# Turning the 64x64 blocks of a triangular inverse one by one instead of two heads at a time

## The chip, the cores and the metric

The kernel runs on one core of a Trainium2 chip. The metric is the device time of one execution in microseconds; of several runs the median is taken. The engines are named as the profile names them: PE is the tensor engine (PEld its weight loads, PE its matmuls), DVE the vector engine, ACT the scalar engine, POOL GpSimd, SP the engine that issues most of the DMAs. Matmuls write to PSUM, which here is eight banks of 128 partitions by 512 float32 columns, named L0 to L3 and Q0 to Q3.

## The reference, cut to what matters

The reference is one transformer block of each of two kinds, applied to 256 tokens of width 1024 in float32. Nearly all of its arithmetic is in products with weight matrices. The change sits in one small part of the first block, the chunked gated delta rule of 8 heads, which solves a lower triangular system for every chunk of 64 tokens:

```python
decay = jnp.exp(jnp.where(causal, gc[..., :, None] - gc[..., None, :], -jnp.inf))
k_beta = k * beta[..., None]
a_low = jnp.where(strict, jnp.einsum("bhnid,bhnjd->bhnij", k_beta, k) * decay, 0.0)
t_mat = a_low + jnp.eye(L, dtype=f32)
rhs = jnp.concatenate([v * beta[..., None], k_beta * jnp.exp(gc)[..., None]], axis=-1)
sol = lax.linalg.triangular_solve(t_mat, rhs, left_side=True, lower=True, unit_diagonal=True)
...
def step(state, inp):
    v_new = u_i - jnp.einsum("bhld,bhde->bhle", w_i, state)
```

The kernel forms the inverse of the unit triangular matrix itself. It works on 128 tokens at once: first the inverses of the two 64x64 blocks on the diagonal, then, in a last level, the 64x64 block below them.

## The kernel before

**Weights.** The work is a fixed list of steps, and every engine's program walks that list. The weights come in units of 128x1024 float32 (512 KB). SP loads a unit into one of four `raw` buffers, ACT casts it to a high part `w_hi` (line 1325), POOL subtracts to get the low part `w_lo` (line 504), and PE multiplies in three products, high by high, high by low, low by high (lines 517 to 519). One unit in the column form is 12 matmuls of 128x512. A semaphore that PE raises tells ACT that a slot may be overwritten.

**Filling.** The small products of attention and of the delta rule depend on each other, with DVE and ACT between them. So PE's program puts weight units between them, by hand: `fill(step, i)` on PE runs the i-th unit of the steps listed for this place. For the inverse of head group 0 (step `("inv", 0)`) these are the units of `("z", 1)` and `("ga", 0)`, for group 1 those of `("gb", 0)` and `("gb", 1)`.

**The inverse.** Each of the two head groups has four heads (`GH`), two tiles of 128 tokens (`NT`, index t), and in each tile two diagonal blocks of 64 rows: partitions 0 to 63 and 64 to 127. `T[partition, t, head, 64]` holds both blocks of a head beside each other in the folded form: the upper partitions hold the second block. `Td` is the same, with each block transposed; `AT` is the transposed matrix itself. The levels l = 1 to 6 double the size of the finished blocks:

1. X = A T: PE, line 1097, sixteen 64x64 matmuls for both tiles (at the last level only the lower block's, eight). DVE masks the result into `X` (line 1910 through a helper; at the last level a plain copy).
2. From level 2 on, `turn_blocks` (line 1079) transposes T on PE, into the other two banks, and ACT copies the result to `Td` (at the last level to the diagonal blocks of `TT`). At level 1 it is instead the other way round, ahead of the loop: `Td` exists first, and the turn gives `T`.
3. A fill: one unit, 12 matmuls; at the last level half a unit, 6 matmuls.
4. PE waits for DVE's `X` and ACT's `TT` mark of this tile, and runs Y = T X (line 1113, sixteen matmuls with `Td` as stationary operand; at the last level line 1110, eight with `TT`).
5. DVE subtracts Y from T (line 1910), and PE's next level waits for it tile by tile.

`turn` is the tensor engine's transpose instruction, `mm` its ordinary matmul. In the kernel before, one turn takes two heads at a time: 128 partitions by 128 columns, of which the 128 columns are two heads of 64. Its result has the first head of the pair in partitions 0 to 63 and the second in 64 to 127, and the two blocks beside each other in the columns. `copy_blocks` on ACT puts this in place by four copies of 64 partitions by 128 elements (line 1609) for a tile.

Of the kernel before, what the change touches and what calls it, by code (L numbers as in the profile page):

```python
# [29 lines left out]
P = 128  # L30
# [5 lines left out]
GH = 4  # L36
# [7 lines left out]
HALF = P // 2  # L44
# [175 lines left out]
def build(nc, a, out, known):  # L220
# [30 lines left out]
    with ctx:  # L251
# [44 lines left out]
        T = big("T", 60, [P, NT, GH, HALF])  # L296
        Td = big("Td", 62, [P, NT, GH, HALF])
        TT = big("TT", 64, TOKENS)
# [20 lines left out]
        h = big("h", 28, [P, NT, D])  # L319
# [46 lines left out]
        ident, tri, ones = square(0), square(1), square(2)  # L366
# [63 lines left out]
        Q = [ctx.enter_context(nc.psum_tensor(f"Q{n}", [P, 512], F32)) for n in range(4)]  # L430
# [8 lines left out]
        AC = Done(scalar_done, known.get("act"))  # L439
# [72 lines left out]
        def _(pe):  # L512
            mm, turn = nc.tensor.matmul, nc.tensor.transpose
# [418 lines left out]
            for step in SCHEDULE:  # L932
                kind = step[0]
                if kind == "u":
# [8 lines left out]
                    for t in range(NT):  # L943
                        for j in range(4):
                            pe.wait_ge(*(VE(step, "scaled", 1, j) if t == 1 and j < 2 else AC(step, "scaled", t, j // 2)))
                            for i in range(2):
                                last = turn(Q[j][:, i * SEQ + t * P:i * SEQ + (t + 1) * P], xn0[:, t, (2 * j + i) * P:(2 * j + i + 1) * P], ident)
# [4 lines left out]
                elif kind == "ba":  # L952

                    pe.wait_ge(*VE(("u",), "split"))
                    for k in range(KD):
                        mm(Q[0][0:16, 0:SEQ], baH[:, k, :], uH[:, k, :], start=k == 0, stop=False)
                        mm(Q[0][0:16, 0:SEQ], baH[:, k, :], uL[:, k, :], start=False, stop=False)
                        last = mm(Q[0][0:16, 0:SEQ], baL[:, k, :], uH[:, k, :], start=False, stop=k == KD - 1)
                    last.then_inc(*PE.mark(step))
                elif kind == "rates":  # L960
                    pe.wait_ge(*VE(("ba",), "turned"))
                    for t in range(NT):
                        last = turn(Q[1][:, t * 16:t * 16 + 16], baT[0:16, t * P:(t + 1) * P], ident[0:16, 0:16])
# [6 lines left out]
                elif kind == "tok":  # L970
                    gr = step[1]
                    for part in range(3):
                        for t in range(NT):
                            b = part * NT + t
# [7 lines left out]
                            for i in range(GH):  # L982
                                last = turn(Q[b % 3][:, i * P:(i + 1) * P], C[:, part * GH + i, t * P:(t + 1) * P], ident)
# [3 lines left out]
                elif kind == "decay":  # L987
# [6 lines left out]
                    for t in range(NT):  # L994
                        last = mm(Q[3][:, t * 8:t * 8 + GH], tri, g[:, t * 8 + gr * GH:t * 8 + gr * GH + GH], start=True, stop=True)
# [6 lines left out]
                elif kind == "feat":  # L1002
# [4 lines left out]
                    src = {"kn": lambda t, i: tok[:, t, 1, i, :], "kb": lambda t, i: kb[:, t, i, :],  # L1007
                           "qn": lambda t, i: tok[:, t, 0, i, :], "qe": lambda t, i: qe[:, i, :]}
                    for b, (what, t) in enumerate(lots):
# [5 lines left out]
                        for i in range(GH):  # L1015
                            last = turn(Q[b % 3][:, i * P:(i + 1) * P], src[what](t, i), ident)
# [4 lines left out]
                    for t in range(NT):  # L1021
                        for i in range(GH):
                            last = mm(Q[2 * t + i // 2][:, (i % 2) * 256:(i % 2 + 1) * 256], kT[:, t, i, :],
                                      kbqT[:, t, i, :, :].rearrange("p a b -> p (a b)"), start=True, stop=True)
# [3 lines left out]
                elif kind == "att":  # L1028
                    gr = step[1]
                    for b in range(4):  # L1030
                        part, pair = b // 2, b % 2
                        pe.wait_ge(*VE(("moba", gr, part), "rope", 1))
                        pe.wait_ge(*VE(("feat", gr), "attn", 1, 1))
                        for i in range(2):
                            for t in range(NT):
                                last = turn(Q[b][:, i * SEQ + t * P:i * SEQ + (t + 1) * P], mtok[:, part, t, 2 * pair + i, :], ident)
# [3 lines left out]
                    for i in range(GH):  # L1040
                        last = mm(Q[0][:, i * P:(i + 1) * P], qTa[:, i, 0:P], kTa[:, i, 0:P], start=True, stop=True)
                    last.then_inc(*PE.mark(step, "scores", 0))
                    for i in range(GH):
                        last = mm(Q[1 + i // 2][:, (i % 2) * SEQ:(i % 2 + 1) * SEQ], qTa[:, i, P:SEQ], kTa[:, i, :], start=True, stop=True)
# [4 lines left out]
                    for b, j in enumerate((0, 1, 2)):  # L1049
# [3 lines left out]
                        for i in range(GH):  # L1053
                            last = turn(Q[b][:, i * P:(i + 1) * P], pr[:, i, j * P:(j + 1) * P], ident)
# [4 lines left out]
                    for i in range(GH):  # L1059
                        bank = Q[3 if i < 2 else 0]  # L1060
                        c0 = (i % 2) * SEQ
                        mm(bank[:, c0:c0 + SEQ], mtok[:, 2, 0, i, :], prT[:, i, 0:SEQ], start=True, stop=False)
                        last = mm(bank[:, c0 + P:c0 + SEQ], mtok[:, 2, 1, i, :], prT[:, i, SEQ:3 * P], start=False, stop=True)
# [4 lines left out]
                elif kind == "inv":  # L1068
                    gr = step[1]
                    fill(step, 0)  # L1070
                    diagonal = [slice(0, HALF), slice(HALF, P)]
# [2 lines left out]
                        return [bank[d, i * HALF:(i + 1) * HALF] for d in diagonal]  # L1074

                    def turn_blocks(bank, src, t):

                        for pair in range(2):
                            last = turn(bank[:, pair * P:(pair + 1) * P], src[:, t, 2 * pair:2 * pair + 2, :].rearrange("p h d -> p (h d)"), ident)
                        return last  # L1080

                    pe.wait_ge(*VE(step, "Td"))
# [4 lines left out]
                    for l in range(1, LEVELS):  # L1087
                        A = [Q[2], Q[3], Q[0], Q[1]] if l % 2 else Q
                        top = l == LEVELS - 1
                        for t in range(NT):  # L1090
                            pe.wait_ge(*(VE(step, "T", l - 1, t) if l > 1 else AC(step, "T", 0, t)))
                            for i in range(GH):
                                for b, d in enumerate(diagonal):
# [3 lines left out]
                                    last = mm(tiles(A[t], i)[b], AT[k, t, i, d], T[k, t, i, :], start=True, stop=True)  # L1097
# [5 lines left out]
                        for t in range(NT):  # L1103
# [3 lines left out]
                            for i in range(GH):  # L1107
                                if top:
                                    d = diagonal[1]
                                    last = mm(tiles(A[t], i)[0], X[d, t, i, :], TT[d, t, i, d], start=True, stop=True)  # L1110
                                else:
                                    for b, d in enumerate(diagonal):
                                        last = mm(tiles(A[t], i)[b], Td[d, t, i, :], X[d, t, i, :], start=True, stop=True)
                            last.then_inc(*PE.mark(step, "Y", l, t))
                elif kind == "scan":
# [4 lines left out]
                    for t in range(NT):  # L1120
                        for i in range(GH):
                            last = mm(Q[t][:, i * P:(i + 1) * P], TT[:, t, i, :], tok[:, t, 2, i, :], start=True, stop=True)
                        last.then_inc(*PE.mark(step, "u", t))
                    for i in range(GH):
                        last = mm(Q[2][:, i * P:(i + 1) * P], kbe[:, i, :], TT[:, 1, i, :], start=True, stop=True)
                    last.then_inc(*PE.mark(step, "wT"))
                    pe.wait_ge(*AC(step, "u", 0))
                    for i in range(GH):
                        last = mm(Q[3][:, i * P:(i + 1) * P], kdec[:, i, :], vn[:, 0, i, :], start=True, stop=True)
                    last.then_inc(*PE.mark(step, "S"))  # L1130
                    for i in range(GH):
                        last = mm(Q[0][:, i * P:(i + 1) * P], aT[:, 0, i, :], vn[:, 0, i, :], start=True, stop=True)
                    last.then_inc(*PE.mark(step, "o", 0))
                    pe.wait_ge(*AC(step, "S"))
                    for i in range(GH):
                        last = mm(Q[2][:, i * P:(i + 1) * P], wT[:, i, :], S[:, i, :], start=True, stop=True)
# [23 lines left out]
                elif kind == "ffn":  # L1160
# [10 lines left out]
                    if c > 0:  # L1171
                        prev = ("ffn", blk, c - 1)
                        pe.wait_ge(*VE(prev, "hidden", 1))
                        for j in range(2):
                            for i in range(2):
                                for t in range(NT):
                                    last = turn(Q[2 * (c % 2) + j][:, i * SEQ + t * P:i * SEQ + (t + 1) * P],  # L1177
                                                hm[:, t, (2 * j + i) * P:(2 * j + i + 1) * P], ident)
# [3 lines left out]
                elif kind == "down":  # L1182
# [5 lines left out]
                    for k in range(KF - TAIL):  # L1188
                        if k == 1:
                            pe.wait_ge(*VE(prev, "hidden", 1))  # L1190
                            for i in range(2):
                                for t in range(NT):
                                    last = turn(Q[0][:, i * SEQ + t * P:i * SEQ + (t + 1) * P], hm[:, t, i * P:(i + 1) * P], ident)
# [17 lines left out]
                elif kind == "in2":  # L1211
# [11 lines left out]
                    elif c == 2:  # L1223
# [9 lines left out]
                        for b in range(2):  # L1233
                            for i in range(2):
# [4 lines left out]
                                          start=False, stop=True)  # L1239
# [66 lines left out]
        def _(act):  # L1306
# [154 lines left out]
            for step in SCHEDULE:  # L1461
# [137 lines left out]
                    last.then_inc(*AC.mark(step))  # L1599
                elif kind == "inv":  # L1600
                    fill(step, 0)
                    diagonal = (slice(0, HALF), slice(HALF, P))

                    def copy_blocks(dst, bank):

                        for odd, a_ in enumerate(diagonal):
                            turned = bank[a_, 0:GH * HALF].rearrange("p (h b d) -> p h b d", h=2, b=2)
                            for b, d in enumerate(diagonal):
                                last = copy(dst(d)[:, odd::2], turned[:, :, b, :])
                        return last  # L1610

                    for t in range(NT):
                        act.wait_ge(*PE(step, "T0", t))
                        copy_blocks(lambda d: T[d, t], Q[t]).then_inc(*AC.mark(step, "T", 0, t))
                    for l in range(1, LEVELS):
                        fill(step, l)
                        if l > 1:
                            for t in range(NT):
                                act.wait_ge(*PE(step, "turned", l, t))
                                bank = Q[t] if l % 2 else Q[2 + t]  # L1620
                                if l < LEVELS - 1:
                                    copy_blocks(lambda d: Td[d, t], bank).then_inc(*AC.mark(step, "TT", l, t))
                                else:
                                    copy_blocks(lambda d: TT[d, t, :, d], bank).then_inc(*AC.mark(step, "TT", l, t))
                    fill(step, LEVELS)
                elif kind == "scan":
                    for t in range(NT):
# [881 lines left out]
```

## Time and profile before

| | us |
|---|---|
| median of 3 runs | 980.59 |
| the three runs | 981.02, 980.59, 980.56 |
| the profiled execution's own time | 981.02 |
| its span in the trace, first to last instruction | 979.2 |
| PE busy in that span | 967.8 (99%) |
| POOL, ACT, DVE busy | 743.4, 528.0, 365.9 |

The page gives the busy time of each engine, the span in 40 slices with the granted clock of the tensor engine, the chain of work that ended last, and groups of instructions by line. The timeline prints instructions in order of start; several of one line that follow each other are merged, with their count, and the time is from the first's start to the last's end. Matmuls overlap: each is shown with its latency, so how fast they run is read from start to start, not from their durations. One float32 matmul in `mm` shows as two records, one `turn` as one.

### The profile page before, as it was taken

Reading aid. Unit: us, or ns where it says so; the run is one execution under the profiler, and the core shown is the slowest. Engines: PE = TensorE matmul, PEld = TensorE weight load, DVE = VectorE, ACT = ScalarE, POOL = GpSimd, SP = SyncE. Lnnn points to the kernel's source line nnn. Section 1 sums busy time; section 2 is a strip of 40 time slices with the busy share of each in tenths; the row PEclk is TensorE's granted clock in tenths of the full one; section 3 lists DMA queues with packets and bytes.
Section 4 is the critical chain, followed back from the end, with each engine's and each line's share of the span. In section 5 each row is a group of like instructions: output and inputs, shape, how many; then the busy total and the mean of one; then the engine's idle time right before and its main releaser. Section 6 shows DMA issues by size and latency. Waiting matters only on the chain.

```text
span 979.2 us, 14799 instructions
## 1 busy us (share of the span) xinstructions
PE 967.8 (99%) x5708; PEld 827.1 (84%) x5708; DVE 365.9 (37%) x842; ACT 528.0 (54%) x827; POOL 743.4 (76%) x593
## 2 busy tenths in 40 slices
PE   8999999999999999999999999999999999999997
PEld 8988879988888888888898887899888888888885
DVE  5687525686534236012122345152252251111103
ACT  5576655465655446465444556585565574444431
POOL 5967643876643988899976987868877789888890
PEclk9999999999999999999999999999999999999999
DMA  7646342555333775767655566645665457666541
GB/s 256 208 139 193 93 124 66 173 154 169 108 109 90 246 245 172 224 192 209 202 159 170 173 207 199 229 151 174 193 191 160 144 172 216 192 185 185 187 132 44
DMA packets 76750, 167.33 MB, mean 171 GB/s; under 512 B 8348, under 2 KB 13704, under 8 KB 76552
## 3 DMA queue, kind: packets, MB, share of 16 engines
q1 hardware_dynamic: 71296, 156.40, 51.8%
q10 hardware_dynamic: 5384, 9.99, 3.3%
q8 instruction: 45, 0.74, 0.3%
q14 instruction: 25, 0.20, 0.1%
HBM read 165.32 MB, written 1.05 MB: 170 GB/s over the span
## 4 chain that ended last, share of the span: by engine, by line
PE 96%; DVE 2%; ACT 1%; issue 0%; DVEq 0%; ACTq 0%
PE L L517 22%; PE L L519 22%; PE L L518 22%; PE Q L519 2%; PE Q L517 2%; PE Q L518 2%; PE L L889 2%; PE L L891 2%; PE L L890 2%; PE Q L1097 1%; PE Q L734 1%; PE Q L1177 1%; PE L L788 1%; PE L L790 1%; PE L L789 1%; PE Q L852 1%
## 5 line engine op out<-in xcount | busy, mean ns | idle before, releaser
L504 POOL TENSOR_TENSOR w_lo<-raw,w_hi 128x512 fp32r<-128x512 f32 x588 | 741.9, 1300 | 212.2 <-ACT w_hi L1325 211.7
L1325 ACT CAST w_hi<-raw 128x1024 fp32r<-128x1024 f32 x294 | 305.0, 1054 | 241.3 <-PE L L519 103.4
L517 PE MATMUL L<-w_hi,uH 128*128 128x512 f32 (+1 forms) x768 | 304.1, 396 | 0.3
L519 PE MATMUL L<-w_hi,uL 128*128 128x512 f32 (+1 forms) x768 | 296.4, 386 | 0.0
L518 PE MATMUL L<-w_lo,uH 128*128 128x512 f32 (+1 forms) x768 | 295.8, 385 | 0.0
L519 PEld LDWEIGHTS L<-w_hi,uL 128*128 128x128 f32 x768 | 144.3, 188 | 29.7
L517 PEld LDWEIGHTS L<-w_hi,uH 128*128 128x128 f32 x768 | 144.4, 188 | 29.1 <-DVE uL L1949 1.5
L518 PEld LDWEIGHTS L<-w_lo,uH 128*128 128x128 f32 x768 | 144.6, 188 | 27.0 <-issue 0.5
L517 PE MATMUL L<-w_hi,hH 128*128 128x512 f32 x176 | 69.0, 392 | 0.0
L519 PE MATMUL L<-w_hi,hL 128*128 128x512 f32 x176 | 68.6, 390 | 0.0
L518 PE MATMUL L<-w_lo,hH 128*128 128x512 f32 x176 | 68.5, 389 | 0.0
L1910 DVE TENSOR_TENSOR hL<-Q,hH 128x512 fp32r<-128x512 f32 x22 | 15.2, 692 | 122.7 <-ACT hH L1766 122.4
L1916 DVE TENSOR_SCALAR small<-small 128x1 f32<-128x1 f32 (+1 forms) x177 | 39.0, 220 | 25.4 <-ACT xv L1683 13.1
L1983 DVE TENSOR_TENSOR L<-L,gA 128x512 f32<-128x512 f32 x19 | 13.3, 700 | 89.9 <-ACT hg L1416 89.5
L1949 DVE TENSOR_TENSOR uL<-Q,uH 128x512 fp32r<-128x512 f32 x28 | 19.3, 692 | 52.9 <-ACT uH L1337 52.9
L1919 DVE SCALAR_TENSOR_TENSOR hm<-L,small,sil 128x512 f32<-128x512 f32 x20 | 15.0, 751 | 64.1 <-PE L L519 63.7
L519 PEld LDWEIGHTS L<-w_hi,hL 128*128 128x128 f32 x176 | 33.0, 188 | 7.0
L517 PEld LDWEIGHTS L<-w_hi,hH 128*128 128x128 f32 x176 | 33.0, 188 | 6.7
L518 PEld LDWEIGHTS L<-w_lo,hH 128*128 128x128 f32 x176 | 33.1, 188 | 6.6
L889 PE MATMUL L<-uH,w_hi 128*128 128x256 f32 x128 | 36.5, 285 | 0.0
L891 PE MATMUL L<-uH,w_lo 128*128 128x256 f32 x128 | 36.2, 283 | 0.0
L890 PE MATMUL L<-uL,w_hi 128*128 128x256 f32 x128 | 36.2, 283 | 0.0
(364 smaller groups left out, 1325.9 us busy)
## 6 DMA issues: line engine op xcount, KB each, us to landing
raw<-in_w_in SPq DMA_DIRECT2D x88, 512.0 KB, 3.7
raw<-in_w_ffn_gate SPq DMA_DIRECT2D x22, 512.0 KB, 3.8
raw<-in_w_ffn_up SPq DMA_DIRECT2D x22, 512.0 KB, 3.7
raw<-in_w_ffn_down SPq DMA_DIRECT2D x22, 512.0 KB, 3.6
raw<-in_w_gate SPq DMA_DIRECT2D x22, 512.0 KB, 3.7
raw<-in_w_up SPq DMA_DIRECT2D x22, 512.0 KB, 3.7
raw<-in_w_down SPq DMA_DIRECT2D x22, 512.0 KB, 3.5
raw<-in_w_out SPq DMA_DIRECT2D x16, 512.0 KB, 3.5
```

The source lines that it names most:

```text
L504: last = nc.gpsimd.tensor_tensor(lo[:, cc], raw[:, n % RAW, cc], hi[:, cc].bitcast(F32), ALU.subtract)
L517: mm(dst, sH, wH, start=start, stop=False)
L518: mm(dst, sH, wL, start=False, stop=False)
L519: return mm(dst, sL, wH, start=False, stop=stop)
L889: mm(bank, sH, uH[:, k, :], start=k == 0, stop=False)
L890: mm(bank, sH, uL[:, k, :], start=False, stop=False)
L891: last = mm(bank, sL, uH[:, k, :], start=False, stop=k == KD - 1)
L1325: copy(halves[SLOT[u]][0], raw[:, u % RAW, :]).then_inc(w_hi_there, 1)
L1910: v(V.tensor_tensor(out_, x_, y_, op), *name)
L1916: v(V.tensor_scalar(out_, x_, s1, s2_, op0, op1), *name)
L1919: v(V.scalar_tensor_tensor(out=out_, in0=x_, scalar=s_, in1=y_, op0=op0, op1=op1), *name)
L1949: vector_next(V.tensor_tensor(uL[:, 4 * half:4 * half + 4, t * P:(t + 1) * P], heads(Q[2 * t + half]), uH[:, 4 * half:4 * half + 4, t * P: ...
```

## The change

It touches step `("inv", gr)` on two engines, and the words of this step only.

On PE, `turn_blocks` no longer transposes two heads at once. It takes each head and each diagonal block by itself: an ordinary matmul with the 64x64 block as stationary operand and the 64x64 corner of the identity as moving operand. Operands and result stay in the same half of the partitions. There are eight of them for a tile where there were two turns. A 64x64 `turn` is not used; it is `mm`.

On ACT, the result now lies as `Td`, `T` and `TT` want it. One copy of 128 partitions by 256 elements takes the place of four for a tile (lines 1607 and 1615 of the new kernel); at the last level two copies of 64 partitions by 256 elements, for the two diagonal blocks of `TT` (line 1618).

```diff
@@ PE, step inv
                     def turn_blocks(bank, src, t):
-
-                        for pair in range(2):
-                            last = turn(bank[:, pair * P:(pair + 1) * P], src[:, t, 2 * pair:2 * pair + 2, :].rearrange("p h d -> p (h d)"), ident)
+                        for i in range(GH):
+                            for b, d in enumerate(diagonal):
+                                last = mm(tiles(bank, i)[b], src[d, t, i, :], ident[d, d], start=True, stop=True)
                         return last
@@ ACT, step inv
-                    diagonal = (slice(0, HALF), slice(HALF, P))
-
-                    def copy_blocks(dst, bank):
-
-                        for odd, a_ in enumerate(diagonal):
-                            turned = bank[a_, 0:GH * HALF].rearrange("p (h b d) -> p h b d", h=2, b=2)
-                            for b, d in enumerate(diagonal):
-                                last = copy(dst(d)[:, odd::2], turned[:, :, b, :])
-                        return last
+                    def blocks(bank):
+                        return bank[:, 0:GH * HALF].rearrange("p (h d) -> p h d", h=GH)
 
                     for t in range(NT):
                         act.wait_ge(*PE(step, "T0", t))
-                        copy_blocks(lambda d: T[d, t], Q[t]).then_inc(*AC.mark(step, "T", 0, t))
+                        copy(T[:, t], blocks(Q[t])).then_inc(*AC.mark(step, "T", 0, t))
...
                                 if l < LEVELS - 1:
-                                    copy_blocks(lambda d: Td[d, t], bank).then_inc(*AC.mark(step, "TT", l, t))
+                                    copy(Td[:, t], blocks(bank)).then_inc(*AC.mark(step, "TT", l, t))
                                 else:
-                                    copy_blocks(lambda d: TT[d, t, :, d], bank).then_inc(*AC.mark(step, "TT", l, t))
+                                    for d in (slice(0, HALF), slice(HALF, P)):
+                                        last = copy(TT[d, t, :, d], blocks(bank)[d])
+                                    last.then_inc(*AC.mark(step, "TT", l, t))
```

PE's program at two of the twelve places where blocks are turned: the one ahead of level 1 of group 0, between two fills, and the one of level 2, behind Y of level 1 and X of level 2. `table` holds the identity; both tiles of tokens are counted together.

```order
 L518 MATMUL L<-w_lo,uH 128x512
 L519 MATMUL L<-w_hi,uL 128x512
-L1079 MATMUL Q<-table,Td 128x128 x4
+L1079 MATMUL Q<-table,Td 64x64 x16
 L517 MATMUL L<-w_hi,uH 128x512
 L518 MATMUL L<-w_lo,uH 128x512
@@ -469,5 +469,5 @@
 L1113 MATMUL Q<-X,Td 64x64 x16
 L1097 MATMUL Q<-T,AT 64x64 x16
-L1079 MATMUL Q<-table,T 128x128 x4
+L1079 MATMUL Q<-table,T 64x64 x16
 L517 MATMUL L<-w_hi,uH 128x512
 L518 MATMUL L<-w_lo,uH 128x512
```

Nothing has changed its place; sixteen small matmuls stand where four turns stood, and that is so at all twelve places (48 turns become 192 matmuls).

ACT's program in the same step, from its first copy to its last, group 0:

```order
-L1609 COPY T<-Q 64x2x64 x8
-L1325 CAST w_hi<-raw 128x1024 x2
-L1609 COPY Td<-Q 64x2x64 x8
-L1325 CAST w_hi<-raw 128x1024
...
-L1609 COPY TT<-Q 64x2x64 x8
+L1607 COPY T<-Q 128x256 x2
+L1325 CAST w_hi<-raw 128x1024 x2
+L1615 COPY Td<-Q 128x256 x2
+L1325 CAST w_hi<-raw 128x1024
...
+L1618 COPY TT<-Q 64x4x64 x4
```

The casts keep their places between the copies; each lot of eight copies has become one of two, or of four at the last level (96 copies become 28).

## Rows read from the trace of the kernel before

**Rows 1.** The page: span, busy time of PE and ACT, the clock granted, the chain.

```profile
span 979.2 us, 14799 instructions
...
PE 967.8 (99%) x5708; PEld 827.1 (84%) x5708; DVE 365.9 (37%) x842; ACT 528.0 (54%) x827; POOL 743.4 (76%) x593
...
PEclk9999999999999999999999999999999999999999
...
PE 96%; DVE 2%; ACT 1%; issue 0%; DVEq 0%; ACTq 0%
```

**Rows 2.** Waits of PE's weight loads, longest first: waiting, waited for, us, times, longest.

```profile
PEld Q L1113 <- issue: 3.5, 10, 0.4
PEld Q L1097 <- DVE T L1910: 2.6, 10, 0.3
PEld Q L947 <- DVE xn L2059: 1.9, 2, 1.1
PEld L L517 <- DVE uL L1949: 1.5, 3, 0.5
```

**Rows 3.** Instructions of line 1079: durations ns min/median/max, first and last start.

```profile
L1079 PE MATMUL Q<-table,T x40: 272/273/332, 126.1 to 294.9; 128*128 128x128 f32 x40
L1079 PE MATMUL Q<-table,Td x8: 270/272/273, 116.4 to 262.4; 128*128 128x128 f32 x8
```

**Rows 4.** PE's timeline around the turn ahead of level 1: start us, us, instruction.

```profile
116.15 0.39 PE L519 MATMUL L<-w_hi,uL 128*128 128x512 f32 x1
116.39 0.60 PE L1079 MATMUL Q<-table,Td 128*128 128x128 f32 x4
116.74 0.48 PE L517 MATMUL L<-w_hi,uH 128*128 128x512 f32 x1
117.05 0.40 PE L518 MATMUL L<-w_lo,uH 128*128 128x512 f32 x1
117.29 0.40 PE L519 MATMUL L<-w_hi,uL 128*128 128x512 f32 x1
```

**Rows 5.** PE's timeline around X of level 1, a run between two fills.

```profile
119.37 0.39 PE L519 MATMUL L<-w_hi,uL 128*128 128x512 f32 x1
119.68 1.15 PE L1097 MATMUL Q<-T,AT 64*64 64x64 f32 x32
120.76 0.50 PE L517 MATMUL L<-w_hi,uH 128*128 128x512 f32 x1
121.10 0.39 PE L518 MATMUL L<-w_lo,uH 128*128 128x512 f32 x1
```

**Rows 6.** The same run of line 1097, without its first six records.

```profile
119.85 0.93 PE L1097 MATMUL Q<-T,AT 64*64 64x64 f32 x26
```

**Rows 7.** Lines 1097 and 1113 over the span: durations ns min/median/max.

```profile
L1097 PE MATMUL Q<-T,AT x352: 218/218/268, 119.7 to 294.3; 64*64 64x64 f32 x176
L1113 PE MATMUL Q<-X,Td x320: 218/218/267, 123.7 to 293.1; 64*64 64x64 f32 x160
```

**Rows 8.** PE's timeline from Y of level 2 to the fill behind the turn of level 3.

```profile
129.10 0.39 PE L519 MATMUL L<-w_hi,uL 128*128 128x512 f32 x1
129.42 1.15 PE L1113 MATMUL Q<-X,Td 64*64 64x64 f32 x32
130.69 1.15 PE L1097 MATMUL Q<-T,AT 64*64 64x64 f32 x32
131.77 0.66 PE L1079 MATMUL Q<-table,T 128*128 128x128 f32 x4
132.18 0.47 PE L517 MATMUL L<-w_hi,uH 128*128 128x512 f32 x1
132.50 0.39 PE L518 MATMUL L<-w_lo,uH 128*128 128x512 f32 x1
```

**Rows 9.** PE's timeline of the last level, group 0; L1110 is Y, tile by tile.

```profile
147.75 1.14 PE L1097 MATMUL Q<-T,AT 64*64 64x64 f32 x16
148.82 0.66 PE L1079 MATMUL Q<-table,T 128*128 128x128 f32 x4
149.23 0.48 PE L517 MATMUL L<-w_hi,uH 128*128 128x512 f32 x1
...
150.80 0.68 PE L1110 MATMUL Q<-TT,X 64*64 64x64 f32 x8
...
151.62 0.65 PE L1110 MATMUL Q<-TT,X 64*64 64x64 f32 x8
```

**Rows 10.** ACT's timeline of the last level, group 0.

```profile
149.30 2.18 ACT L1609 COPY TT<-Q 64x128 f32<-64x128 f32 x8 [2.43 <-PE Q L1079]
```

**Rows 11.** ACT's copies by line: durations ns min/median/max.

```profile
L1609 ACT COPY Td<-Q x64: 257/260/264, 126.5 to 291.2; 64x128 f32<-64x128 f32 x64
L1629 ACT COPY vn<-Q x4: 586/592/616, 155.9 to 301.3; 128x512 f32<-128x512 f32 x4
```

## What the change will do: the prediction

> **What bounds the kernel now.** I read the page first. PE is busy for 967.8 of 979.2 us, its share of the chain that ended last is 96%, and its clock is the higher of its two levels (2.4 GHz) in all forty slices [rows 1]. So the kernel is as long as PE's program, and whatever PE does more or less shows in full unless it falls into one of PE's waits. These waits are the second view: the longest groups are 3.5 us ahead of line 1113, put down to issue, and 2.6 us for DVE's T ahead of line 1097, both in this very stage, ten times each [rows 2]. After them come waits of under 2 us elsewhere. None of the long ones is for a weight part from ACT or POOL, so ACT's time (528.0 us busy) is not what the kernel waits for. The third view is PE's timeline at the places where blocks are turned, since a record's duration is latency and only starts tell the pace: the turns have 272 ns each [rows 3], but four of them and the step to the next matmul take only 0.35 us from start to start (116.39 to 116.74) [rows 4].
>
> **The pace of small matmuls.** The new matmuls have the form of lines 1097 and 1113: 64x64, float32, ordinary, the two diagonal blocks alternating. There are sixteen of them at a place, for both tiles, and sixteen matmuls of that form give 32 records [rows 5, 7]. In a run that is under way, 26 records last 0.93 us from first start to last end; without the 0.22 us of the last one that is 0.71 us for 12 further pairs of records, 0.059 us a pair [rows 6, 7]. So two matmuls of different halves run side by side, and sixteen matmuls in the middle of such a run cost 16 x 0.059 = 0.94 us.
>
> **Term 1, the turn ahead of level 1, twice (one for a group).** It stands between two fills. Before: from the start of the L519 ahead to the start of the L518 behind, 116.15 to 117.05, 0.90 us [rows 4]. The new run stands as X of level 1 stands, between two fills with the same 32 records: 119.37 to 121.10, 1.73 us for the same stretch [rows 5]. That is 0.83 us more each, 1.7 us for two. In it are two steps between forms: 0.31 us from the start of L519 to the first small matmul, and 0.34 us from L517 to L518 behind the run, where neighbours in a fill stand 0.24 us apart (117.05 to 117.29) [rows 4, 5].
>
> The Trainium skill, page "TensorEngine Tiling (Array Packing)", section "Key Properties", says that changing the tiling mode drains the engine. By that rule the change adds one such change in and one out at these two places and none at the others, where a 64x64 run already stands ahead; without it term 1 would be 2 x (0.94 - 0.35) = 1.2 us. The trace agrees with the rule: the longer steps stand just at the switches.
>
> **Term 2, the turns of levels 2 to 6, ten times.** They follow directly on X, a run of 64x64. Before: from the first record of X to the L518 behind the turn, 130.69 to 132.50, 1.81 us [rows 8]. In the new kernel X, turn and fill are one run of 64 records instead of 32, so the stretch is that of level 1, 119.68 to 121.10, 1.42 us [rows 5], plus 0.94 us, 2.36 us. That is 0.55 us more each, 5.5 us for ten. At the last level X has sixteen records of one half only, but it is the same before and after, and the turn behind it is whole.
>
> **Term 3, a wait that goes.** At the last level the fill is only half a unit, and Y comes soon. L1110 starts at 150.80 for tile 0; its eight records have their last start 0.68 - 0.22 = 0.46 us later, and the next was due at 151.32, yet tile 1 starts at 151.62 [rows 7, 9]. ACT's eight copies end at 149.30 + 2.18 = 151.48 [rows 10]: PE waits for them, 0.30 us, and the same pattern stands in group 1. In the new kernel ACT has four copies here. No row shows one of 256 elements; it lies between 260 ns (128 elements) and 592 ns (512 elements) [rows 11], which a straight line makes about 0.37 us. I take that. The turn ends some 0.6 us later than before, about 149.9, and the last two copies then end near 150.7, at the worst (0.59 us each, all four behind that end) at 152.3. PE asks for tile 1 at 151.32 + 0.55 = 151.87. So the wait goes, -0.3 us each, -0.6 us for two; at the worst it stays and 0.1 us more.
>
> **What costs nothing.** ACT's 96 copies of 0.26 us, 25 us, become 28 of about 0.37 us, 10 us. Those 15 us free the engine, but it is not on the path: PE's turn is followed by 12 matmuls of a fill before Y asks for `Td`, and Y's first record follows the last fill matmul by 0.32 us (129.10 to 129.42), the same step as ahead of X of level 1, so it is the change of form and not a late copy [rows 5, 8]. Casts of weights come somewhat earlier, and nobody who sets the end waits for them. What covers the later turn is that same fill, some 2.8 us; the turn is 0.55 us later, and the copies are 1.4 us shorter for two tiles, so the cover grows. Ahead of level 1 the fill is just as long. Queued behind the longer turn on PE is the fill, whose weights are there; who waits for it is ACT, for slots, and that is idle time of an engine with room. DVE's masks of X wait for marks that come before the turn, and T of DVE waits for Y, so the 2.6 us of PE's waits for it [rows 2] stay as they are.
>
> **The sum.** 1.7 + 5.5 - 0.6 = 6.6 us more. Against the profiled execution's own time of 981.02 us (span 979.2 and 1.8 around it) that is 987.6 us; its time is 0.4 us above the median of the runs, so against the median, 980.59, it is 987.2 us. I name 987.2.
>
> **Rival A: the identity matmul is as cheap as a turn.** A turn is one record in the trace, an `mm` is two [rows 3, 7]. If these sixteen matmuls came as sixteen records, a place would cost 0.47 us less: 6.6 - 12 x 0.47 = 1.0 us more, 981.6 us, no difference that a measurement can tell. For it speaks only that the moving operand is an identity as in a turn; against it, that the instruction is the ordinary one, which in lines 1097 and 1113 always shows two.
>
> The Trainium skill, same page, section "Gotcha 2: Feature Incompatibilities", says that column tiling and transpose mode exclude each other for float32. By that the 64x64 form can't have the one-record mode, and this case falls out.
>
> **Rival B: the halves don't run side by side.** X of the last level, with one half only, needs 1.14 us for 16 records where two halves give 32 in 1.15 us [rows 5, 9]. If source, identity or bank kept the pairs apart, each place would cost 0.94 us more: 6.6 + 11.3 = 17.9 us, 998.5 us. Against it: lhs, moving operand and result keep to one half each, exactly as in line 1113.
>
> **Rival C, the other side: ACT's 15 us come back on PE, and the kernel gets faster.** The mechanism would be that a late copy or a late cast ends the steps ahead of Y. All that PE waits ahead of lines 1113 and 1097 is 3.5 + 2.6 us [rows 2]; the chain's share of ACT is 1% [rows 1]. If the whole of it went, 6.6 - 6.1 = 0.5 us more would be left, within 0.2%, and to be faster by over 0.2% another 2.5 us would have to come from casts elsewhere. The point from which it decides is 8.6 us of waits for ACT, where rows show 0.6 us. I give it 2 in 100.
>
> **Rival D: it costs more than the pace says.** 64 records of this form in a row don't occur before; the longest run is 32, after which PE pauses for DVE. Should PE's instructions come too slowly for so dense a run, each place would stall. No row has a price; the nearest are the steps ahead of Y and T, 0.35 us and 0.26 us [rows 2]. Twelve times 0.26 is 3.1 us, which gives 990.3 us.
>
> **How the numbers follow.** The forecast has 0.86, A 0.04, B 0.03, C 0.02, D 0.05. For this kernel 0.2%, some 2 us, is about what a measurement can tell from no change. Slower takes the forecast, B and D, 0.94; same takes A and half of C, 0.05; faster is 0.01. The range is that of the forecast, since the others hold 14 in 100: below, 0.05 us a place in the steps around a run, 0.6 us, and 0.4 us between runs, and some 0.2 us of rounding, 986.0; above, the last level's wait that stays, 0.7 us, the same 0.05 us a place, 0.6 us, and a part of D, 989.2.
>
> **What would show it.** Line 1079 should have 384 records of about 218 ns; the stretch from the L519 ahead to the L518 behind the first turn should read 1.73 us, that from X's first record to the L518 behind 2.36 us, twice and ten times. L1110 of tile 1 should follow tile 0 without a break, ACT's copies should number 28, and PE's busy time should rise by about 7 us, with nothing changed outside the two inverse stages. The prediction is wrong if line 1079 has 192 records (A), if its records stand 0.059 us apart one by one (B), if PE's stretches outside the stages shrink (C), or if gaps open inside the run of 64 (D).

## The result

| | before | changed |
|---|---|---|
| median, us | 980.58 (980.39 to 981.02, 4 runs) | 987.16 (986.13 to 988.43, 4 runs) |
| ratio | 1 | 1.0063, 95% interval 1.0051 to 1.0075 |
| the profiled execution's own time / span, us | 981.02 / 979.2 | 986.18 / 984.4 |
| copies of ACT in the inverse | 96 | 28 |

The kernel is slower by 6.6 us. Most runs of either kernel lie close together, with some up to 3 us above: before and changed kernel were run once more together, and gave 980.39 us (15 runs, 980.11 to 983.63) and 986.38 us (5 runs, 986.19 to 987.25), a difference of 6.0 us. The repetition, expected at about 986.2 us, is the better mean of the two: the ratio of the first comparison, 1.0063, comes to 6.2 us, and all 37 executions of the changed kernel that the first result lists have a median of 986.42 us.

The page of the changed kernel answers [rows 1]. PE has 336 more matmul records and is 6.1 us longer busy; ACT is 15.7 us less busy.

```profile
span 984.4 us, 15403 instructions
...
PE 973.9 (99%) x6044; PEld 832.2 (85%) x6044; DVE 364.5 (37%) x842; ACT 512.3 (52%) x759; POOL 743.1 (75%) x593
...
PE 97%; DVE 2%; ACT 0%; DMA 0%; issue 0%; DVEq 0%; ACTq 0%
```

PE's longest waits are the same as in [rows 2], to a tenth, in the two inverse stages; the third of them, at the start of the kernel (line 947), differs from run to run.

```profile
PEld Q L1113 <- issue: 3.5, 10, 0.4
PEld Q L1097 <- DVE T L1905: 2.6, 10, 0.3
PEld L L517 <- DVE uL L1944: 1.5, 3, 0.5
```

Line 1079 by itself, against [rows 3]: 384 records of 218 ns in place of 48 of 272 ns.

```profile
L1079 PE MATMUL Q<-table,T x320: 218/218/267, 126.0 to 300.3; 64*64 64x64 f32 x160
L1079 PE MATMUL Q<-table,Td x64: 218/218/267, 115.7 to 265.1; 64*64 64x64 f32 x64
```

PE's timeline ahead of level 1, against [rows 4]. From the start of L519 to that of L518 it is now 115.41 to 117.14, 1.73 us, where it was 0.90 us.

```profile
115.41 0.39 PE L519 MATMUL L<-w_hi,uL 128*128 128x512 f32 x1
115.72 1.15 PE L1079 MATMUL Q<-table,Td 64*64 64x64 f32 x32
116.80 0.50 PE L517 MATMUL L<-w_hi,uH 128*128 128x512 f32 x1
117.14 0.39 PE L518 MATMUL L<-w_lo,uH 128*128 128x512 f32 x1
```

PE's timeline at the turn of level 3, against [rows 8]. From X's first record to L518 it is 131.31 to 133.66, 2.35 us, where it was 1.81 us.

```profile
130.03 1.15 PE L1113 MATMUL Q<-X,Td 64*64 64x64 f32 x32
131.31 1.15 PE L1097 MATMUL Q<-T,AT 64*64 64x64 f32 x32
132.29 1.10 PE L1079 MATMUL Q<-table,T 64*64 64x64 f32 x32
133.32 0.50 PE L517 MATMUL L<-w_hi,uH 128*128 128x512 f32 x1
133.66 0.40 PE L518 MATMUL L<-w_lo,uH 128*128 128x512 f32 x1
```

PE's timeline of the last level, against [rows 9]. Two things are new: records of the turn start while the last three of X are still to come, and L1110's sixteen records are one unbroken run of 1.14 us.

```profile
150.10 0.97 PE L1097 MATMUL Q<-T,AT 64*64 64x64 f32 x13
150.86 0.27 PE L1079 MATMUL Q<-table,T 64*64 64x64 f32 x2
150.91 0.22 PE L1097 MATMUL Q<-T,AT 64*64 64x64 f32 x1
150.97 0.22 PE L1079 MATMUL Q<-table,T 64*64 64x64 f32 x1
150.97 0.22 PE L1097 MATMUL Q<-T,AT 64*64 64x64 f32 x1
150.97 0.27 PE L1079 MATMUL Q<-table,T 64*64 64x64 f32 x2
151.03 0.22 PE L1097 MATMUL Q<-T,AT 64*64 64x64 f32 x1
151.03 0.98 PE L1079 MATMUL Q<-table,T 64*64 64x64 f32 x27
151.94 0.50 PE L517 MATMUL L<-w_hi,uH 128*128 128x512 f32 x1
...
153.53 1.14 PE L1110 MATMUL Q<-TT,X 64*64 64x64 f32 x16
```

ACT's copies in the changed kernel, durations ns min/median/max, against [rows 11], and its timeline at the last level, against [rows 10]:

```profile
L1615 ACT COPY Td<-Q x16: 372/372/373, 126.7 to 294.4; 128x256 f32<-128x256 f32 x16
...
151.59 1.51 ACT L1618 COPY TT<-Q 64x256 f32<-64x256 f32 x4 [4.29 <-PE Q L1079]
```

**Where the 5.2 us between the two profiled spans lie.** All matmul records but those of line 1079 are the same in both traces, so their starts can be subtracted pair by pair. The turns ahead of level 1 add 0.81 us each; those of levels 2 to 5 add 0.52 us each, eight times, and the fill behind each of these is 0.03 to 0.07 us longer, some 0.4 us in all; those of the last level add 0.35 us each. L1110 gives back 0.32 us twice, and in the scan, the step behind the inverse, a wait for ACT's copy of vn, 0.3 us once, is gone. That makes 1.6 + 4.2 + 0.4 + 0.7 - 0.6 - 0.3 = 6.0 us by these rounded terms, and 5.9 us read from the starts at both ends of the stretch. The rest of the difference between the spans, some 0.7 us less, arose within the first 12 us of the kernel, where nothing was changed. Of its warm-up matmuls, the twenty records from 3.62 us on took 3.80 us before and 2.95 us in the changed kernel's profile. First the row of before, then that of the changed kernel:

```profile
3.62 3.80 PE L898 MATMUL Q<-C 128*128 128x128 f32 x20
...
3.62 2.95 PE L898 MATMUL Q<-C 128*128 128x128 f32 x20
```

In both traces the step from one of these records to the next falls from 0.213 to 0.111 us, before at 6.6 us and in the changed kernel at 4.8 us. The first granted clock that either trace records, the full one (2.4 GHz), begins within 0.1 us of that moment. What differs is when the tensor engine comes to the higher of its two levels. The page has no clock record for the time ahead of it, and counts that time as full.

### The profile page after: what moved, and what is told of

It reads as the page before. It is cut to its first block, busy times and chain, and to the rows that moved or that the text cites. A ratio compares the mean times of both kernels' runs of the same rounds, so it can differ in the third digit from the quotient of the medians.

```text
span 984.4 us, 15403 instructions
## 1 busy us (share of the span) xinstructions
PE 973.9 (99%) x6044; PEld 832.2 (85%) x6044; DVE 364.5 (37%) x842; ACT 512.3 (52%) x759; POOL 743.1 (75%) x593
## 4 chain that ended last, share of the span: by engine, by line
PE 97%; DVE 2%; ACT 0%; DMA 0%; issue 0%; DVEq 0%; ACTq 0%
PE L L517 22%; PE L L519 22%; PE L L518 22%; PE Q L519 2%; PE Q L517 2%; PE Q L518 2%; PE L L889 2%; PE L L890 2%; PE L L891 2%; PE Q L1097 1%; PE Q L734 1%; PE Q L1079 1%; PE Q L1177 1%; PE L L788 1%; PE L L790 1%; PE L L789 1%
## 5 line engine op out<-in xcount | busy, mean ns | idle before, releaser
L519 PE MATMUL L<-w_hi,uL 128*128 128x512 f32 (+1 forms) x768 | 296.4, 386 | 0.0
L518 PE MATMUL L<-w_lo,uH 128*128 128x512 f32 (+1 forms) x768 | 295.9, 385 | 0.0
L519 PEld LDWEIGHTS L<-w_hi,uL 128*128 128x128 f32 x768 | 144.3, 188 | 29.8
L518 PEld LDWEIGHTS L<-w_lo,uH 128*128 128x128 f32 x768 | 144.6, 188 | 27.1 <-issue 0.5
L519 PE MATMUL L<-w_hi,hL 128*128 128x512 f32 x176 | 68.6, 390 | 0.0
L518 PE MATMUL L<-w_lo,hH 128*128 128x512 f32 x176 | 68.5, 389 | 0.0
L519 PEld LDWEIGHTS L<-w_hi,hL 128*128 128x128 f32 x176 | 33.0, 188 | 7.0
L518 PEld LDWEIGHTS L<-w_lo,hH 128*128 128x128 f32 x176 | 33.1, 188 | 6.6
```

The costliest lines, as they stand in the source:

```text
L518: mm(dst, sH, wL, start=False, stop=False)
L519: return mm(dst, sL, wH, start=False, stop=stop)
```

## The experiments

### Leaving the transpose instruction, in the old form

```diff
-last = turn(bank[:, pair * P:(pair + 1) * P], src[...], ident)
+last = mm(bank[:, pair * P:(pair + 1) * P], src[...], ident, start=True, stop=True)
```

> The kernel before with one word changed: the turns of two heads at a time are made by ordinary matmuls (128x128, identity as moving operand) and no longer by the transpose instruction; ACT's four copies stay. Theory P (PE's program is the kernel; a float32 matmul is two records, a turn is one): each of the 12 places has 8 records some 0.111 us apart in place of 4 at 0.109 us, 0.45 us more, 5.4 us for 12; at the last level Y comes 0.45 us later while the copies come 0.2 us later, so the wait for ACT of 0.30 us goes, -0.6 us: 4.8 us more than before, about 985.4 us. Rival F (the cost of the change lies in the 64x64 form, its count of matmuls and its switches, not in leaving the transpose instruction): under 1 us more than before, below 981.6 us.

Measured: 986.67 us (985.6 to 987.86, 4 runs) against 980.09 us (7 runs), ratio 1.0062, interval 1.0047 to 1.0077. That is about as slow as the changed kernel, with neither 64x64 blocks nor new copies. PE's timeline at the turn of level 3, for [rows 8]:

```profile
130.68 1.15 PE L1097 MATMUL Q<-T,AT 64*64 64x64 f32 x32
131.76 1.16 PE L1079 MATMUL Q<-table,T 128*128 128x128 f32 x8
132.67 0.47 PE L517 MATMUL L<-w_hi,uH 128*128 128x512 f32 x1
132.99 0.39 PE L518 MATMUL L<-w_lo,uH 128*128 128x512 f32 x1
```

Four transposes are four records, four ordinary matmuls of the same size are eight, and the stretch is 2.31 us in place of 1.81 us, 0.50 us more. Subtracting starts as above gives 5.5 us in all behind the opening, where 4.8 us had been expected and the medians differ by 6.6 us: 0.45 us ahead of level 1, 0.50 us at each other place, less 0.23 us at L1110 in each group, where only part of PE's wait went. The spans differ by 4.6 us, since this run too began 0.9 us faster. Rival F has fallen: the cost of the change is that of leaving the transpose instruction. The 64x64 form hardly adds to it: from level 2 on sixteen small matmuls, two side by side, cost what four large ordinary ones cost (0.52 against 0.50 us more); only ahead of level 1, where the small form needs its own switches, is it dearer (0.81 against 0.45 us).

The last level of this run also bears on term 3. ACT's eight old copies are all there, and Y comes later because of the longer turn:

```profile
151.12 2.17 ACT L1609 COPY TT<-Q 64x128 f32<-64x128 f32 x8 [2.95 <-PE Q L1079]
...
152.86 1.23 PE L1110 MATMUL Q<-TT,X 64*64 64x64 f32 x16
```

L1110 takes 1.23 us, against 1.47 us from 150.80 to the end of tile 1 before [rows 9] and 1.14 us without a pause: less than 0.1 us of the wait of 0.30 us is left.

### Every turn made twice

```diff
-for i in range(GH):
+for i in 2 * list(range(GH)):
```

> The changed kernel with every 64x64 turn made twice over, the same result written again: 64 records of line 1079 at a place in place of 32, in runs of 64 (level 1), 96 (levels 2 to 6). Theory P: 16 pairs of records at 0.0585 us more at each of 12 places, 0.94 us each, 11.2 us more than the changed kernel, about 997.6 us. Rival D (PE's instructions come too slowly for long dense runs): gaps inside the runs, clearly more than 12 us. Rival 'launch': the cost of the change lay in the steps between forms and not in the pace: less than 9 us.

Measured: 998.0 us (997.52 to 999.65, 4 runs), ratio 1.0183 to before; 11.6 us above the changed kernel (11.4 us by the starts behind the opening). PE's timeline:

```profile
133.14 1.15 PE L1097 MATMUL Q<-T,AT 64*64 64x64 f32 x32
134.12 2.03 PE L1079 MATMUL Q<-table,T 64*64 64x64 f32 x64
136.08 0.50 PE L517 MATMUL L<-w_hi,uH 128*128 128x512 f32 x1
```

The run of 64 takes 2.03 us where the run of 32 took 1.10 us: 0.93 us for 16 pairs, 0.058 us a pair, at every one of the twelve places. The pace is the measured one, and no gap opens in 96 records without a pause. Rival D has fallen.

### The first turn as before

The turn ahead of level 1 is made with `turn`, two heads at a time, and ACT's four copies; the rest is the changed kernel.

```diff
-turn_blocks(Q[t], Td, t).then_inc(*PE.mark(step, "T0", t))
+turn_pairs(Q[t], Td, t).then_inc(*PE.mark(step, "T0", t))
...
-copy(T[:, t], blocks(Q[t])).then_inc(*AC.mark(step, "T", 0, t))
+copy_blocks(lambda d: T[d, t], Q[t]).then_inc(*AC.mark(step, "T", 0, t))
```

> The changed kernel, with the turn ahead of level 1 made as before (two heads at a time by the transpose instruction, four ACT copies a tile); levels 2 to 6 as changed. Theory P with switches between forms: this place costs 0.81 us less than in the changed kernel, twice, so 1.6 us less, about 984.8 us. A theory of pace alone, without the two steps between forms that this place gained: 2 x (0.94 - 0.35) = 1.2 us less. Rival: all twelve places cost the same, 5.8/12 = 0.48 us, 1.0 us less.

Measured: 984.42 us (984.37 to 984.53, 4 runs), 2.0 us below 986.38 us. The medians alone would not tell 1.6 from 1.2 us; the starts do. Subtracted behind the opening, they give 1.6 us, 0.8 us at each of the two places, and not 1.2 or 1.0 us. The stretch from L519 to L518 is 115.35 to 116.25, 0.90 us again.

```profile
115.35 0.39 PE L519 MATMUL L<-w_hi,uL 128*128 128x512 f32 x1
115.58 0.60 PE L1084 MATMUL Q<-table,Td 128*128 128x128 f32 x4
115.94 0.48 PE L517 MATMUL L<-w_hi,uH 128*128 128x512 f32 x1
116.25 0.40 PE L518 MATMUL L<-w_lo,uH 128*128 128x512 f32 x1
```

### The halves one after the other

```diff
-for i in range(GH):
-    for b, d in enumerate(diagonal):
+for b, d in enumerate(diagonal):
+    for i in range(GH):
         last = mm(tiles(bank, i)[b], src[d, t, i, :], ident[d, d], start=True, stop=True)
```

> The changed kernel with the order inside a turn altered: for each tile first the four heads' blocks of the lower half of the partitions, then the four of the upper half, in place of the two halves in turn. The same 192 matmuls, the same switches. Theory P with side-by-side halves: matmuls start in order, so those of one half follow each other at 0.058 us a record and the two halves can meet only where one half's lot ends and the next begins; a place takes nearly 32 steps in place of 16, 0.7 to 0.94 us more, 8.5 to 11.3 us for 12: 994.8 to 997.6 us. If the engine reorders or overlaps them anyhow, under 2 us more than the changed kernel.

Measured: 990.9 us (990.75 to 991.09, 4 runs), 4.5 us above the changed kernel: between the two expectations.

```profile
132.02 1.15 PE L1097 MATMUL Q<-T,AT 64*64 64x64 f32 x32
133.00 1.49 PE L1079 MATMUL Q<-table,T 64*64 64x64 f32 x32
134.42 0.50 PE L517 MATMUL L<-w_hi,uH 128*128 128x512 f32 x1
```

A turn takes 1.49 us in place of 1.10 us, 0.39 us more, and not 0.7. So the order matters, which shows that in the changed kernel the two halves do run side by side. But strict order is not what holds either. A lot is four matmuls of one half, eight records 0.058 us apart. By these steps each lot begins some 5 ns behind the fifth record of the lot ahead, with three of its records still to come. Here all records have one line number, so which lot a record belongs to is inferred from the steps. The last level of the changed kernel shows the same by line numbers (above): records of line 1079 start ahead of the last three of line 1097, though they stand behind them in the program. Why it is three isn't shown.

### Four copies in place of one

Two versions of the changed kernel with ACT's work as heavy as before. In the first the last level's copies go first to one half of the partitions, then to the other; in the second to both in turn.

```diff
-copy(Td[:, t], blocks(bank)).then_inc(*AC.mark(step, "TT", l, t))
+four(Td[:, t], blocks(bank)).then_inc(*AC.mark(step, "TT", l, t))
...
-last = copy(TT[d, t, :, d], blocks(bank)[d])
+for hs in (slice(0, 2), slice(2, 4)):
+    last = copy(TT[d, t, hs, d], blocks(bank)[d, hs])
```

> The changed kernel with four ACT copies a tile of 64 partitions by 128 elements, in the new layout, in place of one (two at the last level). Theory P with ACT off the path: the eight copies of the last level take 2.18 us from the same start as in the changed kernel, which ends 0.1 us ahead of the moment at which PE asks for tile 1, since Y comes 0.35 us later than before there; no wait, or under 0.1 us, so the time is that of the changed kernel, about 986.4 us, plus at most 0.3 us where the scan waits for ACT's copy of vn. Rival R (the fewer copies took the wait away, as the prediction's third term has it): the wait of 0.30 us at tile 1 of L1110 is back in both groups, +0.6 us. Rival C (ACT's 15 us are worth time on PE): 2 us or more above the changed kernel.

> The changed kernel with four ACT copies a tile, as in act_four_copies, but at the last level too the copies go to the two halves of the partitions in turn, as in the kernel before. In act_four_copies two copies to one half stood behind each other there and started 0.16 us apart in place of 0.27 us, so eight took 1.74 us and not 2.18 us, which blurs the question of the third term. Here they should take 2.18 us again. If Y's later start took the wait away, PE finds tile 1 ready (0.1 us to spare) or waits under 0.1 us, and L1110's records run through in 0.92 to 1.0 us. If the fewer copies took it away, L1110 takes 1.24 us again, as before.

Measured: the first 986.21 us (986.02 to 987.24, 4 runs), the changed kernel's time. The starts subtracted behind the opening give the same time within 0.1 us. So ACT's 15 us are worth nothing here on PE, and rival C has fallen. The second has a single run. Its ACT and PE at the last level:

```profile
153.53 2.17 ACT L1625 COPY TT<-Q 64x128 f32<-64x128 f32 x8 [2.84 <-PE Q L1079]
...
155.48 1.14 PE L1110 MATMUL Q<-TT,X 64*64 64x64 f32 x16
```

Eight copies take 2.17 us, as before, and L1110 runs through all the same: they end at 155.70, and tile 1 is due at 155.48 + 0.46 + 0.06 = 156.00 (the 0.92 and 1.24 us of the expectation are from first to last start; 1.14 us takes in the last record's own 0.22 us). Before, tile 1 started 0.14 us behind the end of the last copy (151.48 to 151.62), so some 0.15 us were to spare. What takes the wait away is that Y comes later behind a longer turn. The copies do have a price one step further on: PE waits for ACT's copy of vn in the scan, 0.33 us before and in mm128, 0.18 us in this run, and nothing measurable in the changed kernel and act_four_copies. Its single time, 988.31 us, isn't used: 1.9 us of what it has above the changed kernel arose in the opening, where the full clock came at 7.5 us, and PE lost 2.6 us to DVE, against some 1.3 us to DVE and ACT in the changed kernel's profile.

### The order of the old copies

The kernel before, with the two loops of `copy_blocks` exchanged.

```diff
-for odd, a_ in enumerate(diagonal):
-    turned = bank[a_, 0:GH * HALF].rearrange("p (h b d) -> p h b d", h=2, b=2)
-    for b, d in enumerate(diagonal):
+for b, d in enumerate(diagonal):
+    for odd, a_ in enumerate(diagonal):
+        turned = bank[a_, 0:GH * HALF].rearrange("p (h b d) -> p h b d", h=2, b=2)
         last = copy(dst(d)[:, odd::2], turned[:, :, b, :])
```

> The kernel before with the two loops of copy_blocks exchanged: the two copies that write one half of the partitions stand behind each other (their sources are the two different halves), where before it was the two that read one half. Same copies, same marks. If it is the written half that lets a copy start early, pairs start 0.16 us apart, eight copies of the last level take 1.74 us, they end 0.4 us earlier, and the 0.30 us wait ahead of tile 1 of L1110 goes: 0.6 us less than before, 979.6 us. If source and target both must stay, all starts are 0.27 us apart as before, and the time is that of the kernel before.

Measured: 980.79 us (10 runs) against 980.23 us (13 runs), ratio 1.0001, interval 0.9991 to 1.0011: no difference. ACT and PE at the last level:

```profile
148.58 2.17 ACT L1609 COPY TT<-Q 64x128 f32<-64x128 f32 x8 [2.46 <-PE Q L1079]
...
150.08 1.47 PE L1110 MATMUL Q<-TT,X 64*64 64x64 f32 x16
```

The copies keep 2.17 us and the pause in L1110 stays (1.47 us in place of 1.14). The same half as target isn't enough.

### The last copies shared with DVE

The kernel before; at the last level tile 1's four copies into TT are DVE's, behind its copies of X, and ACT makes only those of tile 0.

```diff
@@ ACT
-for t in range(NT):
+for t in range(NT if l < LEVELS - 1 else 1):
@@ PE
-pe.wait_ge(*AC(step, "TT", l, t))
+pe.wait_ge(*(VE(step, "diagonal") if top and t else AC(step, "TT", l, t)))
@@ DVE, last level, behind X
+dve.wait_ge(*PE(step, "turned", l, 1))
...
+        v(V.tensor_copy(TT[d, 1, odd::2, d], turned[:, :, b, :]), *((step, "diagonal") if odd and b else ()))
```

> The kernel before with one thing moved: at the last level the four copies of tile 1 into TT are made by DVE, behind its two copies of X, and ACT makes only those of tile 0. Theory (PE waits 0.30 us for ACT's eight copies at tile 1 of L1110, in each group): DVE is free there, its copies take some 0.25 us each and end about 0.6 us before PE asks; the wait goes, 0.6 us less than before, 979.5 us against 980.1 us, and L1110's sixteen records run through in 0.92 us in place of 1.24 us. Rival: the pause of L1110 is not ACT's doing and stays, no change; or DVE's copies, behind X, come late and PE waits as long.

Measured: 979.49 us (979.17 to 981.4, 11 runs) against 980.39 us (980.11 to 983.63, 15 runs), ratio 0.9992, interval 0.9983 to 1.0001. The interval just reaches 1; the trace is clearer. PE, then DVE, at the last level:

```profile
152.15 1.14 PE L1110 MATMUL Q<-TT,X 64*64 64x64 f32 x16
...
150.93 1.26 DVE L2228 COPY TT<-Q 64x128 f32<-64x128 f32 x4 [0.16 <-PE Q L1079]
```

DVE is done at 152.19, and PE asks for tile 1 at 152.67. L1110 runs through. By the starts behind the opening this version is 1.0 us faster than before, where 0.6 us had been expected: 0.32 us at L1110 in each group, and 0.33 us once in the scan, because ACT, four copies lighter, comes sooner to its copy of vn. So the kernel before waited for ACT in two spots of this chain and not in one. It is the fastest version here: the transposes stay, and the copies are shared out where someone waits for them.

## Why the prediction was right, step by step

**What bounds the kernel.** Right: PE's program is the kernel's length. Taking ACT's relief of 15.7 us back moved nothing (act_four_copies), and 0.93 us more of PE work at each place moved the end by 11.6 us (turn_twice). One reading was too simple: the clock is not at the higher level in the whole span, since the first 6.6 us, which the page counts as full, ran at half the pace. The change begins at 116 us, so no term hangs on it.

**The pace.** Predicted 0.059 us a pair of records and 0.94 us a place; measured 0.058 us and 0.93 us.

**Term 1.** Predicted 1.73 us for the stretch; measured 1.73 us, 0.81 to 0.83 us more, twice. The two switches are part of it: first_turn_in_pairs gained 1.6 us by the starts, not 1.2 us.

**Term 2.** Predicted 2.36 us for the stretch; measured 2.35 us at levels 2 to 5. The next fill then took up to 0.07 us longer, which the sum didn't have and no experiment explains. At the last level the step failed that said the turn stands whole behind X: its first five records start beside the last three of X, and the cost was 0.35 us, not 0.55 us. That is 0.4 us of the sum for two groups. "One half only" was loose, too: by the kernel's slices X there reads partitions 0 to 63 and writes 64 to 127, so it shares the partitions it reads with one of the turn's two blocks and those it writes with the other.

**Term 3.** The size was right, 0.32 us against 0.30 us, twice. The argument was not: the prediction had fewer copies take the wait away, since it put ACT's start some 0.6 us later, about as much as Y. But ACT starts when tile 0's part of the turn is done, 1.49 us behind X's first record against 1.55 us before, while Y comes 0.38 us later than before. four_copies_in_turn shows that eight copies are in time behind the changed turn, and in mm128 the old eight cost less than 0.1 us.

**What costs nothing.** Right but for one small thing in the other direction, which the prediction put at nothing: a wait of the scan for ACT's copy of vn, 0.33 us once, is gone in the changed kernel. It went too when four of ACT's copies a group were DVE's (last_copy_shared), stayed whole in mm128, and came back in part, 0.18 us, in four_copies_in_turn.

**The sum.** 6.6 us predicted. The first comparison gave 6.6 us, the repeated one 6.0 us, and the starts of the records 5.9 us. So the agreement of the first median with the forecast to 0.1 us is partly luck. The last level cost 0.4 us less than the sum had, and the scan's 0.3 us were missing from it; some 0.4 us of longer fills went the other way, half of them already covered by 0.55 us a place where 0.52 us was measured. The rest is the spread of four runs: their median stands 0.7 us above that of all 37.

**The rivals.** A (sixteen records a place) didn't occur: there are 384 records, two for each of the 192 ordinary matmuls. The Trainium skill's page "TensorEngine Tiling (Array Packing)", section "Gotcha 2: Feature Incompatibilities", says that transpose mode can't go together with column tiling for float32, and no run here tried a transpose of that form. B didn't occur; the nearest thing tried, lots of one half, cost 4.5 us and not B's 11.3 us, since the lots still overlap by three records. C and D have fallen as told.

## What to carry to other kernels

Where PE sets the length, moving work from an idle engine onto PE costs its full time, however much it tidies: here 68 copies fewer on ACT were bought with 6 us net of PE's time, while sharing out eight copies where PE waits (last_copy_shared) gained 1.0 us by the starts. In these traces a float32 transpose is one record and an ordinary float32 matmul by an identity is two, so look, before changing the shape of a transpose, whether the new shape can still be one. And read what a step costs from start to start, from the last matmul ahead to the second one behind, since switches between forms sit at its edges.

## What the runs showed of the hardware that was not expected

- **Matmuls on other partitions start ahead of their turn.** At the last level three records of line 1097 start behind records of line 1079 that stand later in the program. Line 1097 reads the lower 64 partitions and writes the upper 64 there, and line 1079 goes from lower to lower and from upper to upper in turn. Around 150.97 us three records start within 7 ns; as two records of one of these kinds are some 0.058 us apart elsewhere, they must be of all three. This is worth 0.2 us a place, and it softens a bad order: lots of four cost 0.39 us a place in place of 0.7 to 0.94 us.
- **Copies of 64 partitions on ACT can overlap.** Eight of 64x128 elements, each 0.26 us long, took 2.17 us when the halves took turns, and 1.74 us when source and target half both stayed for two copies (act_four_copies, below). With the source's half alone kept it was 2.18 us (the kernel before), with the target's half alone (copies_by_target) 2.17 us.

```profile
151.41 1.74 ACT L1625 COPY TT<-Q 64x128 f32<-64x128 f32 x8 [2.85 <-PE Q L1079]
```

- **The opening varies with the moment at which the clock rises.** The same twenty records took 3.80 us in one profile and 2.95 us in another; the full clock came at 6.6 and 4.8 us, at 4.2 us in mm128 and at 7.5 us in four_copies_in_turn. PE had been in its warm-up matmuls since 1.3 us each time, and why the moment differs isn't shown. A difference of under 1 us between two spans has to be read from the stage that was changed.
